# One weight chunk per expert loaded by three transfers (112, 8 and 8 partitions) in an encoder layer with a 16-expert feed-forward

## The reference

```
aff, idx = lax.top_k(probs.T, cap)            # each expert picks 64 + 32 tokens
xe = t[idx]
hid = silu(einsum("ecd,edf->ecf", xe, w_gate)) * einsum("ecd,edf->ecf", xe, w_up)
ye = einsum("ecf,efd->ecd", hid, w_down) * aff[..., None]
out = zeros_like(t).at[idx.reshape(-1)].add(ye.reshape(-1, d))
```

## Time and profile before

| | |
|---|---|
| time, median of 3 runs | 2410.2 us (2407.26 to 2411.43) |
| the profiled execution's own time | 2407.7 us |
| its span (first to last instruction) | 2405.8 us |
| PE busy | 2370.5 us, 99% of the span |
| PEld busy | 1625.6 us, 68% |
| DVE, ACT, POOL busy | 1077.1, 519.3, 302.5 us |
| moved by DMA | 707.02 MB, 628.96 of them on SP's queue q1 |
| mean granted TensorE clock | 0.996 |

### The profile page before, as it was taken

One profiled execution on the slowest core, in us unless ns is written; L12 is line 12 of the kernel. 1 busy time (PEld: TensorE's weight loads), 2 busy tenths in 40 slices (PEclk: granted clock), 3 DMA queues, 4 the chain that ended last, 5 costly groups with the idle time before them and its releaser, 6 DMA issues.

```text
span 2405.8 us, 49544 instructions
## 1 busy us (share of the span) xinstructions
PE 2370.5 (99%) x21931; PEld 1625.6 (68%) x21931; DVE 1077.1 (45%) x2059; ACT 519.3 (22%) x1076; POOL 302.5 (13%) x417
## 2 busy tenths in 40 slices
PE   9999999999999999999999999999999999999997
PEld 8888999899898888745655455555555555444454
DVE  7989888888987634451221222122122112212213
ACT  6445444544534412200000000000000000000001
POOL 0422431341341000000000000000000000000001
PEclk9999999999999999999999999999999999999998
DMA  5233234223336545799999999999999999999996
GB/s 187 74 110 123 92 99 134 90 92 118 114 117 212 208 140 207 289 395 410 418 411 420 416 409 420 408 417 409 418 417 408 419 416 409 420 406 416 420 409 259
DMA packets 88646, 707.02 MB, mean 294 GB/s; under 512 B 11824, under 2 KB 16048, under 8 KB 51568
## 3 DMA queue, kind: packets, MB, share of 16 engines
q1 hardware_dynamic: 65504, 628.96, 64.4%
q0 software_dynamic: 14368, 56.80, 7.5%
q10 hardware_dynamic: 8560, 18.10, 2.0%
HBM read 669.76 MB, written 34.06 MB: 293 GB/s over the span
## 4 chain that ended last, share of the span: by engine, by line
PE 47%; DMA 10%; DVE 0%; issue 0%; POOL 0%; POOLq 0%; SPq 0%; ACT 0%; DVEq 0%
PE p_gu L2653 31%; PE p_y L2671 8%; DMA raw<-in_w_e 7%; PE p_y L2674 4%; PE p_z L2674 2%; DMA raw_first<-in_w_e 2%; DMA raw<-xa 1%; PE p_gu L1592 1%; DVE raw L2587 0%; DMA out<-raw 0%; DVE xg L2579 0%; POOLq L2725 0%; POOL out L2489 0%; PE off_banks L1606 0%; SPq L2421 0%
## 5 line engine op out<-in xcount | busy, mean ns | idle before, releaser
L2653 PE MATMUL p_gu<-raw,xT 128*32 128x512 f32 (+1 forms) x8160 | 888.6, 556 | 2.3 <-DMA raw<-in_w_e 2.2
L2653 PEld LDWEIGHTS p_gu<-raw,xT 128*32 128x32 f32 x8160 | 393.8, 110 | 362.8 <-issue 231.0
L2538 DVE SCALAR_TENSOR_TENSOR tg<-tg,p_gu 128x256 f32<-128x256 f32 (+1 forms) x144 | 57.4, 399 | 1051.6 <-ACT tg L2501 1047.1
L2671 PE MATMUL p_y<-raw,hidT 128*32 128x384 f32 x3744 | 433.3, 486 | 0.0
L1282 PE MATMUL pp<-h,wx_hi 128*128 128x256 f32 (+1 forms) x1664 | 423.9, 346 | 0.5 <-ACT fo L836 0.5
L2501 ACT ACTIVATE tg<-p_gu 128x256 f32<-128x256 f32 (+1 forms) x144 | 52.8, 367 | 1266.6 <-PE p_gu L2653 1249.0
L2674 PE MATMUL p_y<-raw,hidT 128*32 128x256 f32 x1248 | 319.5, 379 | 0.0
L1282 PEld LDWEIGHTS pp<-h,wx_hi 128*128 128x128 f32 x1664 | 282.9, 190 | 31.0 <-ACT fo L836 0.7
L1282 PE MATMUL pp<-h,wx_lo 128*128 128x256 f32 (+1 forms) x832 | 281.3, 338 | 0.0
L2674 PEld LDWEIGHTS p_y<-raw,hidT 128*32 128x32 f32 x1248 | 137.2, 110 | 100.1 <-issue 32.1
L2674 PE MATMUL p_z<-raw,hidT 128*32 128x256 f32 x624 | 184.8, 379 | 0.0
(11 more groups left out here) (297 smaller groups left out, 2951.1 us busy)
## 6 DMA issues: line engine op xcount, KB each, us to landing
raw<-in_w_e SPq DMA_DIRECT2D x185, 2048.0 KB, 32.0
raw<-in_w_e SPq DMA_DIRECT2D x58, 1536.0 KB, 32.5
raw_first<-in_w_e SPq DMA_DIRECT2D x23, 2048.0 KB, 33.3
w_raw<-in_w_x SPq DMA_DIRECT2D x48, 512.0 KB, 3.5
dec<-acs POOLq DMA_DIRECT2D x48, 512.0 KB, 4.8
raw<-in_w_e SPq DMA_DIRECT2D x16, 1024.0 KB, 32.6
w_raw<-in_w_g SPq DMA_DIRECT2D x24, 512.0 KB, 3.4
g_tab<-gx POOLq DMA_DIRECT2D x8, 1152.0 KB, 6.0
```

The source lines that it names most:

```text
L2538: dve.scalar_tensor_tensor(out=tg[:, r % 2, 0:w], in0=tg[:, r % 2, 0:w], scalar=1.0, in1=p[:, 0:w], op0=ALU.add, op1=ALU.mult).then_inc(s_ ...
L2653: mm = pe.matmul(p_gu[g][quad(q), 0:w], xT[:, e % 2, k * SLOTS + 32 * g:k * SLOTS + 32 * (g + 1)], slot[:, at:at + w], start=(k == 0), sto ...
L2671: pe.matmul(y_first[half][quad(g), :], hidden(g), w[:, half * 3 * P:(half + 1) * 3 * P], start=first, stop=last)
```

## The change

The first gate-and-up chunk (`i` = 0 of block `b` with `b % 3 == 0`) of each expert from the second on, 15 chunks of 2048 KB, is no longer one transfer of 128 partitions but three: partitions 0 to 111, 112 to 119 and 120 to 127, each 16 KB a partition. Each adds 16 to the slot's semaphore, and PE's wait counts them.

```diff
+PIECES = (slice(0, P - 16), slice(P - 16, P - 8), slice(P - 8, P))
+
+def in_pieces(c):
+    kind, b, i = chunk(c)
+    return c >= RAW and kind == "gu" and i == 0 and b % NB == 0
+
+def landings(c):
+    return sum(16 * (len(PIECES) if in_pieces(n) else 1) for n in range(c % RAW, c + 1, RAW))
...
-    sp.dma_start(raw[c % RAW][:, 0:w], src).then_inc(s_raw[c % RAW], 16)
+    for rows in PIECES if in_pieces(c) else (slice(0, P),):
+        sp.dma_start(raw[c % RAW][rows, 0:w], src[rows, :]).then_inc(s_raw[c % RAW], 16)
...
-                pe.wait_ge(s_raw[c % RAW], (XT_LOADED if c % RAW < EARLY_RAW else 0) + 16 * (c // RAW + 1))
+                pe.wait_ge(s_raw[c % RAW], (XT_LOADED if c % RAW < EARLY_RAW else 0) + landings(c))
```

## The result

The changed kernel takes 2630.1 us (median of 6 runs, 2622.7 to 2664.3) beside 2408.6 us for the kernel before (6 runs): 1.0916 times as long, 95% interval 1.0882 to 1.0951; between the medians it is 221.5 us more. The profiled execution is the longest of the six, 2664.3 us, at a granted clock of 0.966 where the other five have 0.971 to 0.974; the ratio leaves it out, and its rows show more loss than the median has.

A forecast was written before the change was run, and what follows sets the result against it. Bound: PE's pace, then weight chunks landing late because half the DMA engines lag. Waits -4.8 and end -1.6 us sum to -6.4: 2407.7 to 2401.3 profiled, 2403.8 us on the median's side; range 2400 to 2423.

The forecast's parts named there:

- Disturbance: Divided chunks: rows off their usual engine may hinder others; 0 to 1.5 us an expert, taken as nothing.
- The sign that I had named for it: For disturbance: a lower rate in the 5 us of each divided chunk, and waits beginning in the first experts.
- The third rival: Expert stage: disturbance outweighs the relief; at 1.5 us an expert +13.5 us, 2423.7 us; chance 0.14.
- Bound: Expert stage: PE sets the pace until 2001 us, then loses 4.78 us to chunks landing late; SP isn't late.
- rows: Weight chunks: one packet per row of 16 or 12 KB, eight rows per engine, 0.61 us a row.
- issues: SP's queue: 30 more issues of 0.33 us, 0.7 us an expert, hidden by the 30 us before landing.
- The shift and its side: Eight-row transfers load one half of the DMA engines, 0.61 us more per chunk; the early half, three in four.
- the early half: The eight of 16 DMA engines that run dry first near the end, about 21 us ahead of the others.
- the late half: The eight DMA engines still on weights near the end; their pace, 86.69 us an expert, sets when chunks land.
- The waits of -4.8 us: Expert stage: with 0.61 us less per expert on the late half, all PE waits for late chunks go, -4.8 us.
- The end, -1.6 us: After PE's last matmul: `raw<-xa` tiles come earlier, so normalisation ends 4.9 instead of 6.5 us later, -1.6 us.

The follow-up runs named there:

- spread version: Kernel before, whole chunks, plus four eight-row transfers of 8 KB rows per expert (first 15), partitions four apart within 0 to 31: 2428.3 us, ratio 1.0079.
- piled: Kernel before, whole chunks, plus four eight-row transfers of 8 KB rows per expert (first 15), to neighbouring partitions within 96 to 127: 2462.7 us, ratio 1.0218.
- low: Kernel before, whole chunks, plus four eight-row transfers of 8 KB rows per expert (first 15), to neighbouring partitions within 0 to 31: 2463.8 us, ratio 1.0222.
- cross: Kernel before, whole chunks, plus four eight-row transfers of 8 KB rows per expert (first 15), partitions four apart within 64 to 95: 2473.0 us, ratio 1.0268.

## Why the prediction was wrong

**The step that failed** is "Disturbance": "Lower bound nothing", "I take it as the upper bound for an expert" (1.5 us) "and nothing as my value". It measured 14.8 us per divided chunk, ten times the bound; the bytes not moved in the stretches above alone are 8.3 and 11 us. The sign that I had named for it came, waits from the second divided chunk on, but the lower rate lasts 20 us and more instead of 5. The bound came from the wrong row. The gather's 331 GB/s is the rate while rows of another queue are mixed in; it doesn't give the price of rows cut up by partition ranges. With it fell the argument against the third rival: "the full chunks of two halves 21 us apart run at 429 GB/s, so engines out of step don't disturb each other". The row is right and the conclusion doesn't follow: in that row all transfers of weights have 128 partitions, so it can't show what other shapes do. The third rival, which I gave 0.14, had the right effect, a disturbance larger than the relief, and the wrong size, 2423.7 us.

**What costs.** The trace doesn't name the engine of a packet, so own and foreign rest on a pattern. The Trainium skill, "DMA: Bandwidth & Descriptors", section "The descriptor swizzle", has engine 0 write partitions 0 to 3 and 32 to 35 of a transfer of 128 partitions, engine 1 the next four of each, and so on to engine 7, and engines 8 to 15 the same from 64 on. For transfers of 64 and 32 rows I assumed the same shape, scaled to their count, and for 16 and eight rows one row to each engine in order; no row shows it, but the runs agree with it. By it the even and odd partitions and the 32 at a step of four are own throughout, and they cost nothing; the spread version is own too. For the costly ones the same pattern gives an estimate of the rows that are foreign:

| run | foreign rows of 16 KB (of 8 KB at half) | x, added bytes taken off |
|---|---|---|
| even and odd; 32 at step 4 | 0 | 0 |
| piled, low, cross | 16, 14, 16 | 2.3, 2.3, 3.0 |
| 16 rows at step 4 | 64 | 10.3 |
| 16 rows at step 8 | 112 | 13.7 |
| 16 rows at step 7 and the last 16 | 113 | 15.0 |
| 32 contiguous; halves | 120 | 13.8, 13.9 |

(The 1.2 us of the spread version, whose rows are all own, are taken off the other three.) The price rises with the count, 0.14 to 0.19 us a row at first, 0.12 to 0.13 at the end. The change itself isn't in the table: its 16 rows in transfers of eight are all foreign by the pattern, but how the 112 are dealt is unknown; at the table's price, 14.8 us would need nearly all of them foreign too. That the choice of partitions costs is shown by three pairs with equal transfers, rows and bytes: spread and cross, even-odd and halves, 32 at a step of four and in a row. In the first pair even the rows read from memory are the same; in the other two these change with the partitions. That it matters because another engine writes them is inferred: the price follows its count, roughly, in all the runs of the table, but no trace names an engine.

Why a foreign row costs so much is only argued. The Trainium skill, "SBUF — State Buffer", section "Door 1: The DMA port swizzle", has eight partitions behind each of 16 ports. If two engines at one port go at half speed each, the rows behind them in their queues wait as well. Half the rate at a full busy share fits that, and so do rows of 1.129 us instead of 0.615; but no row shows a port, and by the same pattern the piled version sends four rows of a transfer to one port and the cross version one, while the piled one is the cheaper (2.3 and 3.0). The Trainium skill, "SBUF — State Buffer", section "Can I just issue two DMAs to hit both halves?", holds that only one transfer over all 128 partitions can reach all ports. Two transfers of even and odd partitions and four at a step of four ran at 389 and 396 GB/s beside 399 and cost nothing, so in this case the measurement speaks against it.

**The other steps.** *Bound, rows, issues:* right. The chunks' landing sets the time, and SP still waits for slots (977.2 and 375.0 us on its two lines of the earlier trace rows), not the other way round. The changed kernel has 240 packets more than the kernel before (88,886 and 88,646), 16 for each divided chunk: as many as two transfers with eight completions each would add, which agrees with eight rows on eight engines. *The shift and its side:* not settled. By the pattern the spread version adds 1.2 us of rows an expert to eight engines and nothing else. Near its end (columns as in the earlier trace rows):

```profile
2380.00:2385.00 5.00, 5.00 (x72) 2.79 (x68) 0.00 (x0) 0.00 (x0) 0.00 (x0) 1.00 0.98 381
2385.00:2390.00 5.00, 5.00 (x72) 3.00 (x68) 0.00 (x0) 0.00 (x0) 0.00 (x0) 1.00 0.72 250
2390.00:2395.00 5.00, 5.00 (x71) 2.97 (x67) 0.00 (x0) 0.00 (x0) 0.00 (x0) 1.00 0.15 64
2395.00:2400.00 5.00, 5.00 (x70) 2.82 (x66) 2.70 (x8) 0.99 (x3) 0.00 (x0) 1.00 0.13 54
2400.00:2405.00 5.00, 5.00 (x73) 3.26 (x69) 1.19 (x3) 2.53 (x5) 0.76 (x2) 1.00 0.13 52
```

The share no longer stands at 0.5 as in the earlier trace rows; it falls within 10 us to 0.13, two engines of 16, some 15 us behind all others. That would fit eight engines that were the early half, as I had guessed, and have caught up. But the two halves of 64 partitions, which give neither half of the engines more rows, end in the same way:

```profile
2580.00:2585.00 5.00, 5.00 (x72) 3.02 (x68) 0.00 (x0) 0.00 (x0) 0.00 (x0) 1.00 0.21 88
2585.00:2590.00 5.00, 5.00 (x70) 2.85 (x66) 2.88 (x8) 0.99 (x3) 0.00 (x0) 1.00 0.19 74
2590.00:2595.00 5.00, 5.00 (x73) 3.24 (x69) 1.66 (x2) 4.00 (x7) 1.15 (x4) 1.00 0.14 56
```

Even and odd, which cost nothing, keep the 0.5 (0.47 and 0.51 from 2375 to 2385 us). So the end of the spread version doesn't tell which half takes the eight rows. It takes 18.4 us more, the 18 us that bytes on the late half were to cost, where the early half was to cost nothing; whether that is the reason or a coincidence, and what holds up the two engines, stays open.

*The waits of -4.8 us:* never came to be tested, since the disturbance put 180 us of waits in their place. *The end, -1.6 us:* right, as far as it can show. PE's last down matmuls of the changed kernel (first and last start us), and its normalisations in order of time (start us, us):

```profile
L2686 PE MATMUL p_y<-raw,hidT x423: 483/486/510, 2499.8 to 2646.1; 128*32 128x384 f32 x141
```

```profile
2639.35 1.29 DVE L2602 SCALAR_TENSOR_TENSOR raw<-raw,rstdf,nfin 128x1024 f32<-128x1024 f32 x1 [2.05 <-POOL rstdf L2492]
2642.03 2.48 DVE L2602 SCALAR_TENSOR_TENSOR raw<-raw,rstdf,nfin 128x1024 f32<-128x1024 f32 x2 [1.39 <-POOL rstdf L2492]
...
2647.79 3.67 DVE L2602 SCALAR_TENSOR_TENSOR raw<-raw,rstdf,nfin 128x1024 f32<-128x1024 f32 x3
```

PE ends at 2646.6, normalisation at 2651.5: 4.9 us, as forecast, with the first three tiles done before PE's end.

**No version here beats the kernel before.** To unload the late half, rows of its partitions must be carried by the early half, and these are foreign by definition. By an estimate from the table a row moved saves 0.61 / 8 = 0.08 us for each engine of the late half and costs 0.12 to 0.19. That was not tried with a version of its own.

## What to carry to other kernels

When a load is cut into transfers, the choice of partitions can matter more than the number or size of the pieces. Three cuts cost nothing here: by columns, into even and odd partitions, and into four transfers of 32 that go through all 128 partitions at a step of four. Every cut of the 15 chunks into contiguous ranges of partitions cost 207 us or more, and a step alone isn't enough: 16 rows at a step of four or eight cost 154 and 206. As a working rule, not shown, ask whether each partition stays with the DMA engine that writes it in a whole transfer. A divided transfer isn't priced by its own bytes: it can halve the rate of everything in flight around it for 20 us. And a full rate observed while all transfers have one shape says nothing about other shapes; a bound has to come from a row with the same kind of traffic, or be left wide open.

## What was not expected of the hardware

- The DMA engines' busy share stays at 1.0 while the rate halves (220 and 399 GB/s in the same stretch); the share alone would have shown nothing wrong.
- Two transfers of 64 rows cost 0 or 208 us over 15 chunks, four of 32 rows 1 or 207, by the choice of partitions alone.
- The end of the weight loads changes its shape where a version costs time: with the added rows at a step of four two of the 16 engines end some 15 us after the other fourteen, with two halves the busy share is 0.21 to 0.14 for 15 us, and before it stood at 0.5.
- TensorE's granted clock fell from 1.00 to between 0.89 and 0.96 in the stretches with waits and in those right behind them, a mixture of its two levels, 2.4 and 1.2 GHz, and its busy time rose by 81 us with no matmul added.
